# A decoder layer on one core: adaLN modulation sums between other matmuls, subtractions moved from GpSimd to VectorE, and a bias table from shifted columns

## What is computed

```python
mod = (jax.nn.silu(c) @ ada_w + ada_b)[:, None, :]        # c: (1, 2048), ada_w: (2048, 6 * 2048)
sh1, sc1, g1, sh2, sc2, g2 = jnp.split(mod, 6, axis=-1)
h = rms_norm(x, norm1_gain) * (1 + sc1) + sh1
proj = h @ w_in                                           # split in forgetting-attention and NSA columns
...
s_c = einsum(qg, kc) * SCALE + tb[t5_bucket(qpos - cmp_end)]   # NSA, compressed branch: 31 blocks of 32 keys
...
x = x + g1 * (concat(rms_norm(o_fox), rms_norm(o_nsa)) @ w_out)
x = x + g2 * (swiglu(rms_norm(x) * (1 + sc2) + sh2))
```

## Time and profile before

| | before |
|---|---|
| median of 3 runs | 2481.31 us (2481.22 to 2486.51) |
| the profiled execution's own time | 2486.91 us |
| its span | 2485.2 us |
| PE busy | 2411.2 us, 97% |
| DVE busy | 1161.2 us, 47% |
| ACT busy | 693.5 us, 28% |
| POOL busy | 147.0 us, 6% |
| HBM | 320.24 MB read, 133 GB/s over the span |

### The profile page before, as it was taken

The page is one execution under the profiler, slowest core; times in us unless marked ns, Lnnn a source line. Parts: engine busy times, 40 slices in busy tenths (PEclk is TensorE's granted clock), DMA queues, the critical chain, the costliest instruction groups (busy, mean ns, idle before and its releaser), DMA issues.

```text
span 2485.2 us, 27428 instructions
## 1 busy us (share of the span) xinstructions
PE 2411.2 (97%) x10761; PEld 1976.4 (80%) x10761; DVE 1161.2 (47%) x1523; ACT 693.5 (28%) x1001; POOL 147.0 (6%) x109
## 2 busy tenths in 40 slices
PE   7779999999999999999999999999999999999998
PEld 6668787788886688788888888888888888888887
DVE  4885887577727534433333333324233333333334
ACT  4225333433216422332221212222222222222222
POOL 2432110112001100000000000000000000000000
PEclk8889999999969999999999999999999999999999
DMA  9875684476640143233333333333323333333333
GB/s 302 261 267 191 212 287 153 154 274 233 229 142 1 34 169 93 85 94 98 97 93 101 93 99 95 94 100 93 101 93 97 97 94 100 93 101 93 97 98 102
DMA packets 178284, 329.84 MB, mean 133 GB/s; under 512 B 14489, under 2 KB 60287, under 8 KB 177064
## 3 DMA queue, kind: packets, MB, share of 16 engines
q1 hardware_dynamic: 178216, 328.92, 41.3%
HBM read 320.24 MB, written 11.26 MB: 133 GB/s over the span
## 4 chain that ended last, share of the span: by engine, by line
PE 90%; DVE 6%; issue 1%; DMA 1%; ACT 1%; SPq 0%; ACTq 0%; DVEq 0%
PE PS L582 25%; PE PS L584 25%; PE PS L583 25%; DVE acc_first L1292 3%; PE PS L714 2%; PE PS L690 2%; PE PS L589 2%; PE PS L590 2%; PE PS L591 2%; PE PS L823 1%; PE PS L604 1%; PE PS L705 1%; PE PS L572 1%; DMA ada_ring<-in_ada_w 1%; PE PS L810 0%
## 5 line engine op out<-in xcount | busy, mean ns | idle before, releaser
L582 PE MATMUL PS<-hhi,whi 128*128 128x512 f32 x2176 | 856.1, 393 | 9.2 <-DVE hlo L1631 4.2
L583 PE MATMUL PS<-hlo,whi 128*128 128x512 f32 x2176 | 852.6, 392 | 0.0
L584 PE MATMUL PS<-hhi,wlo 128*128 128x512 f32 x2176 | 852.2, 392 | 0.0
L1317 DVE TENSOR_TENSOR wlo<-stage,whi 128x1024 fp32r<-128x1024 f32 x240 | 294.1, 1225 | 860.7 <-ACT whi L986 860.7
L986 ACT ACTIVATE whi<-stage 128x1024 fp32r<-128x1024 f32 x240 | 254.6, 1061 | 1007.4 <-PE PS L584 1007.4
L582 PEld LDWEIGHTS PS<-hhi,whi 128*128 128x128 f32 x2176 | 412.6, 190 | 99.7 <-issue 6.6
L584 PEld LDWEIGHTS PS<-hhi,wlo 128*128 128x128 f32 x2176 | 412.0, 189 | 86.7
L583 PEld LDWEIGHTS PS<-hlo,whi 128*128 128x128 f32 x2176 | 412.2, 189 | 86.4 <-issue 0.7
L980 ACT ACTIVATE whi<-stage 128x1024 fp32r<-128x1024 f32 x144 | 152.7, 1062 | 493.2 <-PE PS L584 387.1
L1264 DVE TENSOR_TENSOR wlo<-stage,whi 128x1024 fp32r<-128x1024 f32 x128 | 162.7, 1272 | 272.2 <-ACT whi L980 272.1
L582 PE MATMUL PS<-ghi,whi 128*128 128x512 f32 x704 | 274.0, 389 | 1.5 <-DVE xT L1655 1.5
(11 more groups left out here) (235 smaller groups left out, 1528.4 us busy)
## 6 DMA issues: line engine op xcount, KB each, us to landing
ada_ring<-in_ada_w SPq DMA_DIRECT2D x128, 512.0 KB, 4.9
stage<-in_ffn_w_gate SPq DMA_DIRECT2D x88, 512.0 KB, 3.6
stage<-in_ffn_w_up SPq DMA_DIRECT2D x88, 512.0 KB, 3.6
stage<-in_ffn_w_down SPq DMA_DIRECT2D x88, 512.0 KB, 3.7
stage<-in_w_in SPq DMA_DIRECT2D x80, 512.0 KB, 5.9
ada_first<-in_ada_w SPq DMA_DIRECT2D x64, 512.0 KB, 5.2
stage<-in_w_out SPq DMA_DIRECT2D x32, 512.0 KB, 3.8
xnat<-in_x SPq DMA_DIRECT2D x4, 1024.0 KB, 7.9
```

Source lines behind the costliest of these rows:

```text
L582: mm(PS[:, b, :], whi[:, slot, kk, cols], rhi, start=start, stop=False)
L583: mm(PS[:, b, :], whi[:, slot, kk, cols], rlo, start=False, stop=False)
L584: return mm(PS[:, b, :], wlo[:, slot, kk, cols], rhi, start=False, stop=stop)
L1317: v.tensor_tensor(wlo[:, j % NW, :, :], stage[:, j % NSTAGE, :, :], whi[:, j % NW, :, :].bitcast(F32), ALU.subtract).then_inc(w_lo, 1)
```

## The change

It makes five edits.

1. **Four of the 16 row blocks go to TensorE.** DVE adds up blocks 0 to 11 only (`FIRST_DVE = 12`). The last four are multiplied on TensorE by 16 matmuls of one column a stage (`direct`, weights are the blocks of `ada_first[3]`, the moving column is that of `silu_c`). Column sums of `acc_first` (`sums`) stay 8 a stage. The sums of stage j + 1 stand between the tiles of stage j: the 16 in six places of tiles 1 to 3 of group 0, the 8 after the two halves of the first tile of group 1. `acc_first` has four buffers, and s = 3 is loaded before s = 2, after TensorE has used it.
2. **No tensor work on POOL in the opening.** `wlo` is made by DVE there as everywhere; `xn` is gone: DVE makes `h1t` directly as x times scale times the row factor, ACT adds the shift and rounds in one instruction, and `h_low` adds the shift itself.
3. **The bias table.** Instead of 55 matmuls of 8 columns there are 8 (`lags`, one for each distance of 128), kept in SBUF. In NSA 16 matmuls of 56 columns with a shifted identity (`shift`) give `cmp_bias` in PSUM bank 6, and ACT copies it. The trip through DRAM is gone.
4. **The sums of components 4 and 5** leave their place ahead of the compression products, where `bias_table()` now stands, and go one by one behind the value matmuls of NSA steps 8 to 15 (four a step). DVE adds their bias after the last step.
5. POOL makes `shift` when the last projection is done.

The core of the diff:

```diff
-                for s in range(4):
-                    if j >= 1:
-                        sp.wait_ge(first_acc, KT * (j - 1) + 4 * (s + 1))
+                for s in (0, 1, 3, 2):
+                    if j >= 1 and s < 3:
+                        sp.wait_ge(first_acc, FIRST_DVE * (j - 1) + 4 * (s + 1))
+                    elif j >= 1:
+                        sp.wait_ge(first_pe, j)
...
-            bias_columns(range(CBW // 2))
+            pe.wait_ge(xt_sb, 8 + 3)
+            for i in range(NLAG):
+                c0 = NREV + P * (NLAG - 1 - i)
+                n = min(P, NREV + NFWD - c0)
+                last = mm(PS[0:n, 2, NH * i:NH * (i + 1)], onehot[:, c0:c0 + n], relb[:, :], start=True, stop=True)
+            last.then_inc(line_pe, 1)
...
+                def direct(j, ns):
+                    for i in ns:
+                        n, kk = i // 4, i % 4
+                        last = mm(PS[:, 7 if j else 5, n:n + 1], ada_first[3][:, kk, n // 2, P * (n % 2):P * (n % 2 + 1)],
+                                  silu_c[:, FIRST_DVE + kk:FIRST_DVE + kk + 1], start=kk == 0, stop=kk == 3)
+                    if 15 in ns:
+                        last.then_inc(first_pe, 1)
+                def sums(j, ns):
+                    for n in ns:
+                        for half in range(2):
+                            last = mm(PS[:, 7 if j else 5, 4 + n:5 + n],
+                                      acc_first[:, 2 * (j % 2) + half, P * n:P * (n + 1)],
+                                      ones[:, 0:1], start=half == 0, stop=half == 1)
+                    if 3 in ns:
+                        last.then_inc(mod_pe, 1)
...
-            modulation_sums()
+            bias_table()
...
-                values(UF + step - 1, lambda kb, c0=2 * P * win + P * kv: nv[:, kb, c0:c0 + P],
-                       win == 0, False).then_inc(pv_done, 1)
+                if step == NH:
+                    pe.wait_ge(pct_sb, 2)
+                    pe.wait_ge(ada_acc, ADA_STEPS)
+                sums = range(4 * (step - NH), 4 * (step - NH) + 4) if NH <= step < 2 * NH else None
+                values(UF + step - 1, lambda kb, c0=2 * P * win + P * kv: nv[:, kb, c0:c0 + P], win == 0, False,
+                       (lambda kb: modulation_sum(sums[kb])) if sums else None).then_inc(pv_done, 1)
...
-                    f(h1t[:, k % 4, :], xn[:, k, :], ACT.Identity, bias=mod[:, 0, k:k + 1],
-                      scale=mod[:, 1, k:k + 1]).then_inc(h_full, 1)
...
-                    f(hhi[:, k, :], h1t[:, k % 4, :], ACT.Copy).then_inc(h_hi, 1)
+                    f(hhi[:, k, :], h1t[:, k % 4, :], ACT.Identity, bias=mod[:, 0, k:k + 1]).then_inc(h_hi, 1)
...
+                for k in (2 * j, 2 * j + 1):
+                    if k >= 4:
+                        dve.wait_ge(h_lo, k - 3)
+                    v.scalar_tensor_tensor(out=h1t[:, k % 4, :], in0=xt0[:, k, :], scalar=mod[:, 1, k:k + 1],
+                                           in1=ssf[:, :], op0=ALU.mult, op1=ALU.mult).then_inc(h_full, 1)
...
-                g.tensor_tensor(xn[:, k, :], xt0[:, k, :], ssf[:, :], ALU.mult).then_inc(xn_done, 1)
...
-                    g.tensor_tensor(wlo[:, c % NW, :, :], stage[:, c % NSTAGE, :, :],
-                                    whi[:, c % NW, :, :].bitcast(F32), ALU.subtract).then_inc(w_lo, 1)
```

More of the change, by code:

```diff
@@ L593, in first_groups @@
             def first_groups():
-                def shift_and_scale(j):
-                    pe.wait_ge(first_acc, KT * (j + 1))
-                    if j == 0:
-                        pe.wait_ge(bank_free[7], 1)
-                    if j >= 2:
-                        pe.wait_ge(part_out, j - 1)
-                    for n in range(2 * CK):
-                        for half in range(2):
-                            last = mm(PS[:, 7, n:n + 1], acc_first[:, half, P * n:P * (n + 1)], ones[:, 0:1],
-                                      start=half == 0, stop=half == 1)
-                    last.then_inc(mod_pe, 1)
@@ L706, in transposes, with values @@
                     last.then_inc(t_pe, 1)
-            def values(u, v_of, start, stop):
+            def values(u, v_of, start, stop, beside=None):
                 pe.wait_ge(t_act, 2 * (u + 1))
@@ L715, in values @@
                               start=start and kb == 0, stop=stop and kb == 3)
+                    if beside is not None:
+                        last = beside(kb)
                 return last
@@ L805, in cmp_transposes, with modulation_sum, bias_table @@
                 last.then_inc(pct_pe, 1)
-            def modulation_sums():
-                pe.wait_ge(ada_acc, ADA_STEPS)
-                for n in range(2 * KT):
-                    last = mm(PS[:, 7, 128 + n:129 + n], acc[:, n // KT, P * (n % KT):P * (n % KT + 1)],
-                              ones[:, 0:1], start=True, stop=True)
-                last.then_inc(mod3_pe, 1)
+            def modulation_sum(n):
+                return mm(PS[:, 7, n:n + 1], acc[:, n // KT, P * (n % KT):P * (n % KT + 1)], ones[:, 0:1],
+                          start=True, stop=True)
+            def bias_table():
+                pe.wait_ge(pads, 1)
+                for s in range(8):
+                    o = PS[:, 6, 7 * NH * s:7 * NH * (s + 1)]
+                    near = 96 - CS * s
+                    low, high = (near + P, 1), (near, 0) if near >= 0 else (near + 2 * P, 2)
+                    for c0, i in (low, high):
+                        last = mm(o, shift[:, c0:c0 + P], lags[:, i:i + 7, :].rearrange("p i h -> p (i h)"),
+                                  start=i == 1, stop=i != 1)
+                last.then_inc(table_pe, 1)
             pe.wait_ge(norm_done, 28)
             nsa_scores(0, 0)
-            modulation_sums()
+            bias_table()
             pe.wait_ge(unf, 4)
@@ L1268, in h_low @@
                 dve.wait_ge(h_hi, k + 1)
[L1269 to L1270 removed]
+                v.scalar_tensor_tensor(out=hlo[:, k, :], in0=h1t[:, k % 4, :], scalar=mod[:, 0, k:k + 1],
+                                       in1=hhi[:, k, :].bitcast(F32), op0=ALU.add, op1=ALU.subtract).then_inc(h_lo, 1)
             def partial_out(j):
```

216 lines of the change are left out of this document (126 added, 90 removed).

## The result

The changed kernel takes 2444.7 us (median of four runs, 2444.1 to 2448.6) against 2482.4 us (2481.2 to 2486.5) for the kernel before: a ratio of 0.985, 95% interval 0.983 to 0.987, 37.7 us less. The forecast was 2454.8 and its range 2443 to 2475. So it went the way that was said, and 10 us further.

A forecast was written before the change was run, and what follows sets the result against it. TensorE was busy 2411 of 2485 us; in the opening its column sums waited for DVE's accumulation. Opening -25.3, start of NSA -6.7, sums beside values +5.5 gave -26.5 us: 2454.8 us, range 2443 to 2475.

The forecast's parts named there:

- The start: Up to the opening's first tile: with eight look-ups left, it starts at 46.6 instead of 53.1, 6.5 us earlier.
- The clock in stage 0: Opening's first stage: cost until the full clock returns; lower end 2 us, upper end 12.5, taken as 5.
- A stage: Opening, each later stage: TensorE's 16.1 us and the loop through DVE meet, 16.6 us instead of 19.0.
- Whether the clock stays up: Opening after stage 0: granted clock stays at 1.00, as in an earlier pause of about 3 us followed by eight sums.
- Contention: Opening: DVE's accumulations take 0.67 us each with POOL silent, against 1.87 with POOL's `wlo` and `xn` running beside them.
- the fourth rival: Opening: transfers, not POOL, made DVE slow, so only the start is won; 2474 us, chance 0.05.
- the transfers did not set the pace: Denies the first rival: opening's ten transfers a stage take 18.7 us, 15 us less gain; 2469.5 us, chance 0.18.
- third rival: Opening: one-column products between tiles hold the clock down, stages of about 22.9 us; 2506 us in all, chance 0.08.
- the second rival: Clock returns in stage 0 after 4 us and weight loads hide; 10 us more gain, 2444.8 us, chance 0.2.
- The table: Start of NSA: 16 table products of 4.6 us replace 32 sums of 11.34 us, 6.7 us less.
- The compression products: Start of NSA, behind the table: they follow at 0.43 us each as before, no gain.
- The sums beside the values: NSA value steps: 32 sums cost 3.4 to 6.7 us, taken as 5.5; steps 0.6 to 0.8 us longer.

The follow-up runs named there:

- Run 8: Kernel before without its second piece of 28 look-ups, so half of the bias table is left out: 2481.0 us, ratio 0.9988.
- run 7: Changed kernel with the opening's 16 `wlo` operations back on POOL: 2460.7 us, ratio 0.989.
- run 6: Kernel before with the opening's 16 `wlo` operations moved from POOL to DVE, nothing else: 2470.6 us, ratio 0.994.
- run 9: Changed kernel with 4 of the 16 direct products a stage, the other twelve left out (modulation incomplete): 2428.6 us, ratio 0.977.
- run 1: Changed kernel with the 32 one-column sums back in one piece ahead of the table and compression products: 2466.1 us, ratio 0.992.
- run 2: Changed kernel with the 32 sums in one piece right behind the compression products: 2451.6 us, ratio 0.987.
- run 3: Changed kernel with the 32 sums ahead of the table, and twelve unread 256-column products between table and compression products: 2458.3 us, ratio 0.990.
- run 4: Kernel before with only the 32 sums spread over the value steps, four a step: 2479.3 us, ratio 0.9985.
- run 5: Kernel before with the 32 sums spread over the value steps and 16 unread 56-column products ahead of the compression products: 2474.2 us, ratio 0.995.
- run 10: Changed kernel with unread 128-column products between look-ups, first direct products and sums, and fourteen in the wait for h: 2449.3 us, ratio 0.986.
- run 11: Changed kernel with the 16 sums of component 5 moved from the value steps into the wait for sub-layer 2's row factor: 2442.5 us, ratio 0.9831.
- run 12: Changed kernel with both the edits of run 10 and run 11: 2445.5 us, ratio 0.9845.

## Why the forecast held, and where it did not

- **The start**, -6.5 forecast. The first tile is at 45.49, not 46.6. The 1.1 is that of the first look-up, at 28.22 for 29.4; the later steps fit: the direct products 6.8 us for 6.6, the sums 3.5 for 3.5. Run 8 bears out the size for the second look-ups. The forecast put the fall of the clock at 32.7, which its own row (0.82 over 32 to 34) places at 33.3; here it fell at 30.6, ahead of the first direct product, so that all sixteen paid the lower level.
- **The clock in stage 0**, 5 taken. It cost 2.1 (19.2 - 17.1), the lower end. But the upper end is real: run 7 met it with one disturbed tile. No row of before could tell which of the two it would be.
- **A stage**, 16.6 forecast, 17.1 measured. Two terms are too small. TensorE's own work is 16.8, not 16.1: a product between tiles is 0.227, not 0.211, with what it adds to its neighbour, which is 0.4 of the 0.7; the rest is not taken apart. And the forecast ended the loop at "the next h is ready"; in fact two accumulations and `partial` stand behind `hlo` on DVE, and the first direct products wait for `partial`, 0.3 us a stage. Over the opening the misses cancel: -1.1 for the start, -2.9 for the clock in stage 0, +2.4 for the seven intervals (the last of them was only 16.0), +0.8 for the last stage. That 179.0 meets 179.8 so closely is in part luck.
- **Whether the clock stays up**: right, 1.00 from 52 us on. The row that the forecast drew on shows less than it said: the pause in it is 1.8 us (2.18 of 4 busy), not about 3.
- **Contention**: right. DVE's accumulations took 748 ns in place of 1076, and run 6 shows that POOL was the cause and not the transfers, which excludes the fourth rival.
- **Rivals**: the transfers did not set the pace at 17.1; run 9 shows them as next, at a mean stage of 15.35. The products between the tiles did not hold the clock down once it was up (third rival): the windows from 52 us on stand at 1.00. In stage 0 of run 7 they did what it says, once. The measured 2444.7 is also the number of the second rival, 2444.8, but not its mechanism: the clock did come back early in stage 0 (2.1), and no loads hid, neither in the stages nor beside the values. The missing gain came from the compression products, so the match is luck.
- **The table**: -7.7 for -6.7. The clock never fell, so all sixteen products took 0.23.
- **The compression products**: the failed step. "The compression products follow at 0.43 as before" took the price of a row as belonging to the product. It belonged to the clock that the sums ahead had left. Runs 1, 2 and 3 show it by putting sums, or wide work, ahead or behind. The forecast had even written down the fall 2.5 us into the sums and then removed the sums without asking what would follow. Also missing was that this needs something in the way of the wait for the first weights (runs 4 and 5); the forecast costed that wait at nothing, and in the changed kernel the table's 3.7 us stood in its place.
- **The sums beside the values**: +5.4 for +5.5, and the agreement is luck. A step with four sums takes 6.25 us (scores from 751.19 to 757.44) where one took 5.41 (786.40 to 791.81), 0.84 more, outside the 0.6 to 0.8 that the forecast named and the upper end of its cost: nothing hides. What was given back is at the end: the last stretch, up to the last `probcT` product, takes 13.4 us (790.35 to 803.72) where it took 14.2 (832.02 to 846.24), four sums included, because TensorE waits 3.0 us for `probT` and not 3.9 and the clock is back sooner behind the wait.

Forecast and result agree to 10 us in the median because all stretches but one hold, two of them by misses that cancel; the one that does not is larger than the distance.

## What to carry to other kernels

Before you move or remove a block of narrow matmuls, read the granted clock at its end: here the narrow work behind it ran at what it left. Then ask which wait the block had covered. Put one-column work between wide tiles, or behind a row of narrow products and ahead of a wide one, and not ahead of the row. Where the critical loop passes through DVE, look for POOL work with tensors in SBUF at the same time; moving it to the busier DVE can be a gain, as in run 6.

## What was not expected of the hardware

- Products of 62 columns in fp32, 64 in a row, took 14.4 to 14.5 us in every trace in which they started at the full level (the changed kernel, runs 2, 3, 5, 7, 9 to 12) and 26.3 to 27.6 in every one in which the level fell ahead of them or at their start (before, runs 1, 4, 6, 8). Those of 56 columns did the same: 3.68 and 7.05 for sixteen. It is no rule for every narrow row: sixteen products of 31 columns in the changed kernel began at the full level behind a wait of 0.94 us, and the clock fell within them, 4.54 us for the 3.66 of the next such row. The scores behind paid for it, 4.61 us for 2.32:

```profile
690.03 4.54 PE L828 MATMUL PS<-kc,nq 128*128 128x31 f32 x32 [0.94 <-DVE kc L1607]
694.39 4.61 PE L720 MATMUL PS<-nk,nq 128*128 128x512 f32 x8
```

- Full tiles with a few one-column products between them ran at either level: 1.00 from 52 us to the end of the opening in the changed kernel, where three half tiles had run without a wait ahead of the first such product; 0.50 from 51 to 70 us in run 7, where a wait of 1.06 us stood behind the first half tile.
- A 128-column fp32 product after every two one-column ones did not keep the clock up (run 10: 0.50 from 32 to 50 us, with PE never idle); fourteen of them alone had it back before their 5.0 us were over.
